# Two projection units ahead of modulation chunks 1 and 3, VectorE's loads first, squares in halves

## What is computed

```python
D_MODEL, SEQ, CTX_LEN, DEPTH, N_MOD = 1024, 512, 256, 2, 6

def rms_norm(x, g):
    y = x * lax.rsqrt(jnp.mean(x * x, axis=-1, keepdims=True) + EPS)
    return y * g

def modulate(x, g, shift, scale):
    return rms_norm(x, g) * (1 + scale) + shift
...
# per layer, for the latent tokens (c) and the context tokens (c_ctx):
mod = silu(c) @ w_mod[l] + b_mod[l]        # 6 x 1024: shift, scale, gate for mixer and MLP
a = modulate(x, norm1_g[l], shift1, scale1)
p = a @ w_in[l]                            # 1024 -> 2304
...                                        # windowed attention, retention, Fourier mixing
x = x + gate1 * (concat(heads) @ w_out[l])
x = x + gate2 * squared_relu_mlp(modulate(x, norm2_g[l], shift2, scale2))
```

## Time and profile before

| what | us |
|---|---|
| median of three runs | 1704.47 (1702.3 to 1705.03) |
| the profiled execution | 1702.21 |
| its span | 1700.4 |
| TensorE busy | 1606.9 |
| VectorE busy | 1042.7 |
| ScalarE busy | 588.5 |
| GpSimd busy | 584.6 |

### The profile page before, as it was taken

How to read it: one execution, slowest core, us unless ns; L and a number is a source line. 1 busy time by engine, 2 the same in 40 slices (tenths; PEclk the granted TensorE clock), 3 DMA queues, 4 the chain that set the end, 5 groups by cost and what they waited for, 6 DMA issues and landing times.

```text
span 1700.4 us, 23038 instructions
## 1 busy us (share of the span) xinstructions
PE 1606.9 (94%) x8800; PEld 1365.0 (80%) x8800; DVE 1042.7 (61%) x1481; ACT 588.5 (35%) x951; POOL 584.6 (34%) x324
## 2 busy tenths in 40 slices
PE   6899989989999999999899988998999799999998
PEld 2788878978888888888788887887897688888887
DVE  5778966868765767566466776585544544444442
ACT  4522435652532221211212345234662432332321
POOL 1336661012333222233222443336003444444442
PEclk9899999989999999999999999999999899999999
DMA  9333111105333434344343432231002132333332
GB/s 325 101 126 118 51 44 50 51 9 154 94 99 116 120 112 131 99 142 133 91 143 103 129 110 75 71 91 38 1 1 82 55 99 88 97 95 90 99 99 87
DMA packets 168653, 162.33 MB, mean 95 GB/s; under 512 B 6624, under 2 KB 132208, under 8 KB 168560
## 3 DMA queue, kind: packets, MB, share of 16 engines
q1 hardware_dynamic: 168560, 161.02, 31.1%
HBM read 158.90 MB, written 2.10 MB: 95 GB/s over the span
## 4 chain that ended last, share of the span: by engine, by line
PE 57%; issue 25%; DVE 7%; POOL 4%; ACT 4%; DMA 1%; SPq 1%; POOLq 0%; DVEq 0%; ACTq 0%
PE psA L1931 17%; PE psB L1931 16%; POOL Wlo L525 4%; PE psA L1711 2%; PE psA L1712 2%; PE psA L1713 2%; PE psB L1711 2%; PE psB L1713 2%; PE psB L1712 2%; PE ps L1903 2%; DVE Ab L1438 1%; PE psS L1713 1%; PE psS L1712 1%; PE psS L1711 1%; PE psS L1572 1%
## 5 line engine op out<-in xcount | busy, mean ns | idle before, releaser
L525 POOL TENSOR_TENSOR Wlo<-raw,Whi 128x1024 fp32r<-128x1024 f32 x158 | 384.5, 2434 | 829.8 <-ACT Whi L663 829.8
L663 ACT ACTIVATE Whi<-raw 128x1024 fp32r<-128x1024 f32 x181 | 191.4, 1059 | 635.0 <-PE psB L1931 269.4
L1438 DVE TENSOR_TENSOR Ab<-Tb 128x512 f32<-128x512 f32 (+2 forms) x68 | 167.9, 2469 | 175.9 <-ACT Tb L929 175.8
L1931 PE MATMUL psA<-Ahi,Whi 128*128 128x512 f32 (+1 forms) x432 | 138.1, 362 | 11.4 <-issue 5.0
L1931 PE MATMUL psB<-Ahi,Whi 128*128 128x512 f32 (+1 forms) x424 | 135.1, 362 | 2.6 <-POOL Wlo L529 2.2
L1931 PE MATMUL psA<-Ahi,Wlo 128*128 128x512 f32 (+1 forms) x432 | 137.5, 361 | 0.0
L1931 PE MATMUL psA<-Alo,Whi 128*128 128x512 f32 (+1 forms) x432 | 136.8, 359 | 0.0
L1931 PE MATMUL psB<-Ahi,Wlo 128*128 128x512 f32 (+1 forms) x424 | 134.9, 361 | 0.0
L1211 DVE SCALAR_TENSOR_TENSOR X<-psB,modT,X 128x256 f32<-128x256 f32 (+1 forms) x104 | 67.1, 664 | 109.7 <-PE psB L1931 109.6
L1931 PE MATMUL psB<-Alo,Whi 128*128 128x512 f32 (+1 forms) x424 | 134.3, 359 | 0.0
L1931 PE MATMUL psA<-Hhi,Whi 128*128 128x512 f32 (+1 forms) x368 | 117.7, 362 | 14.1 <-DVE X L1211 12.8
(11 more groups left out here) (331 smaller groups left out, 3525.9 us busy)
## 6 DMA issues: line engine op xcount, KB each, us to landing
raw<-in_w_ff_dram SPq DMA_DIRECT2D x135, 512.0 KB, 4.1
modraw<-in_w_mod_dram SPq DMA_DIRECT2D x72, 512.0 KB, 4.3
raw<-in_w_in_dram SPq DMA_DIRECT2D x36, 512.0 KB, 3.7
modst<-in_w_mod_dram SPq DMA_DIRECT2D x16, 512.0 KB, 5.8
raw<-in_w_out_dram SPq DMA_DIRECT2D x16, 512.0 KB, 4.3
modat<-in_w_mod_dram SPq DMA_DIRECT2D x8, 512.0 KB, 3.8
macc<-in_w_ff_dram SPq DMA_DIRECT2D x5, 512.0 KB, 3.5
modraw<-in_dft_lat_dram SPq DMA_DIRECT2D x8, 257.0 KB, 3.6
```

What stands on the lines that cost most here:

```text
L525: nc.gpsimd.tensor_tensor(Wlo[:, s, :], raw[:, s, :], Whi[:, s, :], ALU.subtract).then_inc(S["lo_done"], 1)
L663: nc.scalar.activation(whis[slot], raws[slot], ACT.Copy).then_inc(S["hi_done"], 1)
L1438: V.tensor_tensor(Ab[:, k % 2, c0:c1], Tb[:, k % 2, c0:c1], Tb[:, k % 2, c0:c1], ALU.mult).then_inc(S["h_full"], 1)
L1931: last = mm(dst[:, c0:c1], wt, x[:, i, c0:c1], start=f, stop=e)
```

## The change

TensorE's and VectorE's order is rewritten at the start of layer 0. TensorE spreads the root right after the sums of chunk 2, runs projection unit 0, then P4 to P7, then half of unit 1, the turn of row 1 and the sums of chunk 3, then the rest. VectorE runs D0 to D4, chunk 2's reduce, a new addition of the half sums, D5, the gain, the reciprocal, tiles 0 to 3, D6, D7, chunk 3's reduce and gain, tiles 4 to 7. The spread's banks ps6 and ps7 are needed for chunks 1 and 3, so ScalarE copies the spread to SBUF (`sq_flat`) between its parts of tiles 0 and 1, and tiles 2 to 7 read the copy. Loads come as D0, P0, ... D3, P3, then D4 to D7, then P4 to P7; the raw weights of units 0 and 1 are loaded after the eighth, and the last three loads stand behind the small tables. ScalarE squares 512 columns at a time, twelve squares in place of six. GpSimd's program is not changed.

```diff
+    FIRST = [(("DVE", "PE")[i % 2], i // 2) for i in range(8)] + [("DVE", i) for i in range(4, 8)] + [("PE", i) for i in range(4, 8)]
...
-    sq_junk, mod_row = sq_flat[:, 0:D], sq_flat[0:2, D:D + MCH]
+    sq_junk, mod_row, mod_acc = Ab[:, :, :].rearrange("p a b -> p (a b)"), scr[0:2, 2, :], scr[:, 0:2, :]
...
             if i >= NST:
-                before = i - NST
-                sp.wait_ge(S[("mod_first", "mod_pe")[before % 2]], before // 2 + 1)
-            w = 8 * (1 - i % 2) + i // 2
+                engine, n = FIRST[i - NST]
+                sp.wait_ge(S["mod_first" if engine == "DVE" else "mod_pe"], n + 1)
+            w = FIRST[i][1] + (8 if FIRST[i][0] == "DVE" else 0)
...
-        for i in range(16):
+        for i in range(13):
             first_mod(i)
...
-            if i in (11, 13):
-                w_load(i // 2 - 5, i // 2 - 5, r2(i // 2 - 5), proj_src(0, i // 2 - 5), True)
+            if i == 7:
+                for u in range(2):
+                    w_load(u, u, r2(u), proj_src(0, u), True)
...
         tmp_load(0)
+        for i in range(13, 16):
+            first_mod(i)
...
+            if n == 0:
+                act.wait_ge(S["ss_ready"], 1)
+            sums = psS[:, t0:t1] if n else ssq[:, :, 2]
...
+            nc.scalar.activation(sq_junk[:, n % 3 * 512:n % 3 * 512 + 512], Xin[:, t, half * 512:half * 512 + 512], ACT.Square, accum_out=ssq[:, t, half:half + 1]).then_inc(S["ss_half"], 1)
...
+        x_copy(0)
+        x_copy(1)
+        x_square(0, 0)
+        x_square(1, 0)
+        x_copy(2)
+        x_copy(3)
+        for t in range(2, NT):
+            x_square(t, 0)
+        for t in range(4):
+            x_square(t, 1)
+        x_copy(4)
+        x_square(4, 1)
         x_copy(5)
-        x_square(1)
+        x_square(5, 1)
         row_copy(0)
         x_copy(6)
-        x_square(2)
         x_copy(7)
-        for t in (3, 4, 5):
-            x_square(t)
         nc.scalar.activation(warm[:, :], epst[:, :], ACT.Sqrt).then_inc(S["stat_done"], 1)
         norm_root(0)
         hi_static(0)
         hi_static(1)
+        norm_hi(0, 0)
+        act.wait_ge(S["a_full"], 2)
+        nc.scalar.activation(sq_flat[:, 0:LAT], ps6[:, :], ACT.Copy)
+        nc.scalar.activation(sq_flat[:, LAT:COLS], ps7[:, 0:COLS - LAT], ACT.Copy).then_inc(S["rb_copied"], 1)
+        for k in range(1, 4):
+            norm_hi(0, k)
         row_copy(1)
...
                 hi_static(u0 + u + 2)
+                if l == 0 and u == 0:
+                    for k in range(4, KT):
+                        norm_hi(0, k)
...
-                                              in1=(ps6, ps7)[s][:, 0:c1 - c0], op0=ALU.mult, op1=ALU.mult)
+                                              in1=sq_flat[:, c0:c1] if n == 0 and j >= 2 else (ps6, ps7)[s][:, 0:c1 - c0], op0=ALU.mult, op1=ALU.mult)
...
-        for i in range(6):
+        for i in range(5):
             start(i)
         mod_reduce(0, 2, 0)
         shifts(0)
-        start(6)
-        norm_root(0)
-        start(7)
+        dve.wait_ge(S["ss_half"], 2 * NT)
+        V.tensor_tensor(ssq[:, :, 2], ssq[:, :, 0], ssq[:, :, 1], ALU.add).then_inc(S["ss_ready"], 1)
+        start(5)
         dve.wait_ge(S["mod_evac"], 2)
         gain(0, 0, 0, 4)
-        shifts(1)
+        norm_root(0)
         dve.wait_ge(S["x_ready"], KT)
         norm_full(0, 0)
         norm_full(0, 1)
-        mod_reduce(0, 3, 1, 2, (psS[:, 0:512], psS[:, 512:1024]))
+        dve.wait_ge(S["rb_copied"], 1)
+        norm_full(0, 2)
+        norm_full(0, 3)
+        for i in range(6, 8):
+            start(i)
+        shifts(1)
+        mod_reduce(0, 3, 1)
         dve.wait_ge(S["mod_evac"], 4)
         gain(0, 0, 4, 8)
-        for j in range(2, KT):
+        for j in range(4, KT):
             norm_full(0, j)
...
         mod_sums(S["mod_first"], 3, 3, macc)
-        for i in range(4, 8):
-            first_mod(i)
         pe.wait_ge(S["mod_evac"], 2)
         spread(0)
-        turn_row(1)
-        pe.wait_ge(S["mod_evac"], 3)
-        mod_sums(S["mod_first"], 7, 7, Ab, 2, (psS[:, 0:512], psS[:, 512:1024]))
...
-                    if l == 0 and u == 0 and t == NL:
-                        pe.wait_ge(S["mod_evac"], 4)
+                    if l == 0 and u == 1 and t == 3:
+                        turn_row(1)
+                        pe.wait_ge(S["mod_evac"], 3)
+                        mod_sums(S["mod_first"], 7, 7, mod_acc)
...
+                if l == 0 and u == 0:
+                    pe.wait_ge(S["rb_copied"], 1)
+                    for i in range(4, 8):
+                        first_mod(i)
```

More of the change, by code:

```diff
@@ L754, in x_copy, with x_square @@
             nc.scalar.activation(X[:, m, :], pair[m % 2][:, 0:COLS], ACT.Copy).then_inc(S["x_ready"], 1)
-        def x_square(t):
+        def x_square(t, half):
             if t == 0:
-                act.wait_ge(S["xa_in"], 16 * NT)
-                act.wait_ge(S["xb_in"], 16 * NT)
-            link(nc.scalar.activation(sq_junk, Xin[:, t, :], ACT.Square, accum_out=ssq[:, t, 0:1]))
+                act.wait_ge(S[("xa_in", "xb_in")[half]], 16 * NT)
+            n = NT * half + t
+            if n >= 3:
+                act.wait_ge(S["ss_half"], n - 2)
+            nc.scalar.activation(sq_junk[:, n % 3 * 512:n % 3 * 512 + 512], Xin[:, t, half * 512:half * 512 + 512], ACT.Square, accum_out=ssq[:, t, half:half + 1]).then_inc(S["ss_half"], 1)
         def row_copy(c):
@@ L767, in row_copy @@
                 act.wait_ge(S["row_turned"], c)
[L768 to L772, removed]
+            nc.scalar.activation(mod_row, (psS[0:2, 0:512], ps6[0:2, :])[c], ACT.Copy).then_inc(S["row_copied"], 1)
+        x_copy(0)
[10 more added lines that the diff above has]
+        x_square(4, 1)
         x_copy(5)
-        x_square(1)
+        x_square(5, 1)
         row_copy(0)
         x_copy(6)
-        x_square(2)
         x_copy(7)
-        for t in (3, 4, 5):
-            x_square(t)
         nc.scalar.activation(warm[:, :], epst[:, :], ACT.Sqrt).then_inc(S["stat_done"], 1)
@@ L788, in _ @@
             u0, uf = BASE[l], BASE[l] + UP + UO
-            if l == 0:
-                for k in range(KT):
-                    norm_hi(0, k)
             tiles = proj_tiles(l)
@@ L1060, in mod_unit_lat, with mod_reduce @@
                 .then_inc(used, 1)
-        def mod_reduce(l, chunk, g, streams=2, banks=(ps6[:, :], ps7[:, :])):
+        def mod_reduce(l, chunk, g, streams=2):
             dve.wait_ge(S["modp_ready"], g + 1)
             for s in range(streams):
-                V.tensor_reduce(modT[:, l, bass.ds(chunk * 4, 4), s], banks[s].rearrange("p (t k) -> p t k", t=4),
+                V.tensor_reduce(modT[:, l, bass.ds(chunk * 4, 4), s], (ps6, ps7)[s][:, :].rearrange("p (t k) -> p t k", t=4),
                                 axis=AX, op=ALU.add).then_inc(S["mod_red"], 3 - streams)
@@ L1579, in mod_sums @@
                 for t in range(4):
-                    last = tr(banks[s][:, t * P:(t + 1) * P], acc[:, s, t * P:(t + 1) * P])
+                    last = tr((ps6, ps7)[s][:, t * P:(t + 1) * P], acc[:, s, t * P:(t + 1) * P])
             last.then_inc(S["modp_ready"], 1)
@@ L1629, in first_mod @@
         def first_mod(i):
-            c, part, slot = i // 4, i % 4, (2 * i + 1) % NST
-            pe.wait_ge(modst_in[slot], 16 * ((2 * i + 1) // NST + 1))
+            c, part, at = i // 4, i % 4, FIRST.index(("PE", i))
+            slot = at % NST
+            pe.wait_ge(modst_in[slot], 16 * (at // NST + 1))
             for kk in range(2):
-                last = mm(psS[0:2, 512 * c:512 * c + 512], csil[:, 2 * part + kk, :], modst[:, slot, kk * MCH:(kk + 1) * MCH],
+                last = mm((psS[0:2, 0:512], ps6[0:2, :])[c], csil[:, 2 * part + kk, :], modst[:, slot, kk * MCH:(kk + 1) * MCH],
                           start=(part == 0 and kk == 0), stop=(part == 3 and kk == 1))
@@ L1641, in turn_row @@
             for t in range(4):
-                last = tr(psS[:, 512 * c + 2 * t:512 * c + 2 * t + 2], mod_row[:, t * P:(t + 1) * P], 2)
+                last = tr((psS, ps6)[c][:, 2 * t:2 * t + 2], mod_row[:, t * P:(t + 1) * P], 2)
             last.then_inc(S["row_turned"], 1)
```

12 lines of the change are left out of this document (6 added, 6 removed).

## The result

| kernel | median, us | ratio to before, 95% interval | profiled span |
|---|---|---|---|
| before | 1703.51 (1702.3 to 1705.03, four runs) | | 1700.4 |
| changed | 1720.76 (1719.65 to 1727.65, four runs) | 1.0108 (1.0084 to 1.0132) | 1717.9 |

A forecast was written before the change was run, and what follows sets the result against it. TensorE, busy 94% of the span, was taken as the bound; -0.15 (early norm), +7.2 and +1.9 (TensorE work), +11.7 (hole) and +2.7 (clock) made +23.4 us on 1702.21, so 1725.6, range 1712 to 1731.

The forecast's parts named there:

- T: Start of the second k, the second step of TensorE's first projection unit: 51.25 before, forecast 51.1, 0.15 us earlier.
- row units P4 to P7: On TensorE behind unit 0: four row units, before hidden in the wait for the norm, add 7.2 us.
- hole before unit 2: TensorE idle from 78.6 to 90.3, 11.7 us, for unit 2's Wlo behind the norm's odd low parts on GpSimd.
- low clock in unit 2: After the idle stretch TensorE runs at clock 0.50 for a while: 2.7 us more, bounds 0 and 5.4.
- the fourth operation of D5 waits for the first low part, and the gain for the second: VectorE before the reciprocal: held by GpSimd's low parts until 39.5 and about 42.0; first normalised tile at 43.9.
- Rival A: VectorE and GpSimd do not meet before the norm: second k at 46.5, 4.6 us earlier, time 1721; chance 0.26.
- Tile 7's hold: VectorE's tile 7, both operands in SBUF, meets GpSimd's low part of tile 5: +1.8 us, between 0 and 1.85.
- Paid to the end, unless something later swallows it.: TensorE is full behind unit 2, 60.00 busy us of 60, so a shift of unit 2 reaches the end.
- rival B: Later TensorE waits swallow part, or unit 2 keeps the full clock: 1717, with more of it 1712; chance 0.12.
- Rival D: Early norm is the whole effect: second k at 44.4, row units covered by later VectorE waits, 1695; chance 0.02.
- C: Longer hole: last load or ScalarE queue late, or low clock lasts twice, 1728 to 1732; chance 0.08.
- E: Nothing changes, because an earlier second k, near 28, cancels the rest; chance 0.02.

The follow-up runs named there:

- experiment 2: The changed kernel with GpSimd's first two low parts of weights held until VectorE's reciprocal is done: 1717.03 us, ratio 1.0092.
- experiment 3: The changed kernel with the matmuls of P4, P5 and P6 left out, their loads kept: 1716.44 us, ratio 1.0090.
- Experiment 1: The changed kernel with unit 2's low weights moved on GpSimd ahead of the low parts of tiles 5 and 7: 1719.16 us, ratio 1.0110.
- experiment 11: The changed kernel with GpSimd's low part of tile 5 held until VectorE has multiplied all eight tiles: 1719.9 us, a single time.
- experiment 8: The changed kernel run again, unedited: 1720.60 us, ratio 1.0117.
- Experiment 7: The kernel before with half squares, tiles 0 and 1 ahead of D7, spread ahead of P7, GpSimd's first low parts behind the reciprocal: 1701.85 us, ratio 1.0000.
- experiment 6: The kernel before with GpSimd's first low parts held until D7 is done and the spread ahead of P7: 1698.47 us, ratio 0.9987; repeated, 1697.82.

## Why the prediction was right, and where its sizes were off

The terms, at the start of unit 3 and then at the end:

| term | predicted | measured |
|---|---|---|
| T | -0.15 | -1.46 (51.25 to 49.79) |
| unit 0 from T | 0 (10.2) | -0.68 (9.52) |
| row units P4 to P7 | +7.2 | +6.96 |
| turn, wait and sums in unit 1 | +1.9 | +2.03 (10.19 - 8.16) |
| hole before unit 2 | +11.7 | +11.25 |
| low clock in unit 2 | +2.7 | +1.78 (9.94 - 8.16) |
| sum at unit 3 | +23.4 | +19.88 |
| later | 0 | -2.4 |
| at the end | +23.4 | +17.5 |

The time measured is 4.8 us below the predicted 1725.6, with the mechanism as forecast: the first tile late in spite of an early root, the row units and the sums in the open, the hole with GpSimd's Wlo as releaser, the low clock behind it. The loss itself was missed by more: +23.4 against +17.3 between the medians. The forecast started from the profiled execution of before (1702.21), which lies 1.3 below the median of 1703.51, and that hid part of the miss by luck. Nearly all the terms were too high.

**T.** The step "the fourth operation of D5 waits for the first low part, and the gain for the second" happened as put: 4.82 and 2.30 us, and with GpSimd out of the way 2.73 and 0.16 (experiment 2). The Trainium skill, in "SBUF — State Buffer" (SBUF: two separate sides), says that the loser of the shared port pair is blocked for the whole instruction; the 128x8 operation of 2.30 us agrees. Mis-sized was the start: a half square took ScalarE 0.61 us, not 0.7, its eighth copy ended at 31.6, not 32.3, the root came at 33.6, not 34.6, and the first tile at 42.5, not 43.9. Rival A is answered by experiment 2: the meeting cost about 4 us, where I had put 4.6.

**Row units, turn and sums.** Both terms held within 0.3 us, and experiment 3 shows that they are paid one for one. P7's load cost nothing.

**The hole.** Its length of 11.7 was right within 0.5, its place came 2.1 us earlier, because all ahead of it did. Experiment 1 shows that GpSimd's order makes it. It also shows what my step left out: with the Wlo moved, 5.5 us come back at 152 us, not the whole 11, since unit 2 then waits for tiles 4 and 5, which come just as late, and the wait for ScalarE follows. The weights and the tiles are both late; removing one wait uncovers part of the other. That the tiles are late because chunk 3 is summed inside unit 1 is read from the traces; no run moved the sums forward.

**Tile 7's hold, +1.8.** 1.6 on VectorE, and 1.15 to 1.6 of the path (experiment 11): right in kind, its price a little too high.

**The clock, +2.7.** I took the price from the stretch behind T in before; the low level there lasted 5.6 us from T, here 3.6 from the end of the hole: eight matmuls, 1.78. The same error, with the other sign, sits in unit 0: its low level ended 3.9 us after T, sooner than in before, and it took 9.52 instead of 10.2. Together these two are 1.6 of the 3.5 us missed at unit 3; T is 1.3.

**"Paid to the end, unless something later swallows it."** This step failed in part; it was rival B on a small scale. 2.4 us came back. Some of it can be seen: TensorE's wait for the context Fourier tables, first before, then changed:

```profile
229.12 2.05 PE L1783 MATMUL psS<-modraw,Pu 128*128 128x129 f32 x16 [2.24 <-DMA modraw<-in_dft_ctx_dram]
```

```profile
248.46 2.05 PE L1811 MATMUL psS<-modraw,Pu 128*128 128x129 f32 x16 [1.73 <-DMA modraw<-in_dft_ctx_dram]
```

That is 0.5 us; three waits between before's 262 and 267 (3.97 us in sum, 3.41 after the change) give another 0.6. About 1 us comes after 450 us, where runs of one kernel differ by more. How much comes back is itself not firm: in the repeat (experiment 8) the same table wait was 0.96, and of 20.8 us at unit 3 15.2 were left at the end. That part of the delay comes back is seen in both traces; its size is not settled.

**Rival D** (the early norm is the whole effect) asked for T at 44.4 and cover for the row units. T came at 49.79, and nothing later on VectorE paid the row units back. Experiment 7 tried the early norm with the row units kept where they were, and even there it gave 1.2 us at 152 and nothing in the median. Of the others, C (a longer hole, up to 1732) and E (no change) did not happen either.

## What to carry to other kernels

When a producer is moved later, read the helper engine's program order around it. Here GpSimd stood idle for 25 us, in the last ten with ready work behind a wait, and half of that hole's price lay in its order alone. Work that stood in a wait of the bounding engine was free there and cost its full length where that engine had no wait; ask which chain ends the wait before filling or emptying it. And before making an engine start earlier, look at whom it then meets: two small edits, which only keep GpSimd out of VectorE's way and turn two steps round, gave the version that came out ahead of both kernels, if only by some 2 us over the one before.

## What was unexpected on the chip

- An operation on 128x8 took 2.30 us beside GpSimd's subtraction, 0.16 alone. Its own size says nothing about what it can lose.
- VectorE's casts, with a single SBUF input, were held as well: 1.82 and 2.33 us (experiment 11), where the changed kernel shows 0.21 and 0.29 for the same two:

```profile
82.29 0.21 DVE L1228 CAST identr<-ident 128x128 fp32r<-128x128 f32 x1
82.54 0.29 DVE L1230 CAST maskr<-maskf 128x256 fp32r<-128x256 f32 x1
```

- Once in the MLP of layer 0 TensorE stands still with no releaser that the profile shows, and the length differs between runs: 5.03 us in before, 6.40 in the changed kernel, 5.57 and 5.89 in the two runs of experiment 6's version:

```profile
813.95 0.80 PE L1931 MATMUL psA<-Ahi,Whi 128*128 128x512 f32 x2 [5.03 <-issue]
```

The first 3.1 us of it are a wait for GpSimd's low part of the next weights, the same in all thirteen traces; what differs is the rest. In twelve of the thirteen traces TensorE starts again 1.3 to 1.5 us after the second of two transfers of instructions (16384 bytes each, on queue 8) has landed: at 812.45 in before and 829.62 in the changed kernel. In experiment 3, where TensorE's program is six matmuls shorter, it does not wait for that transfer, and GpSimd's Wlo ends the gap:

```profile
825.32 0.61 PE L1958 MATMUL psA<-Ahi,Whi 128*128 128x512 f32 x2 [3.50 <-POOL Wlo L529]
```

So the rest looks like a wait for the engine's own program. No experiment was made on it, and that stays an inference. It is large enough to hide a gain of 2 us in one profile.
